# A bidirectional chunked scan: sharing one score product between the two directions

## What is computed

```python
xd = x * dt[..., None]                              # inputs, per head
a_cs = cumsum(dt * a)                               # within a chunk, per head and direction
decay = exp(where(tri, a_cs[:, None] - a_cs[None, :], -inf))
cb = einsum("bclgn,bcsgn->bclsg", cc, bc)           # scores: per group, no direction in them
y_diag = einsum("bclgr,bcsgrp->bclgrp", cb * decay, xd)
states = einsum("bclgn,bclgr,bclgrp->bcgrpn", bc, exp(a_cs[-1] - a_cs), xd)
h = h * exp(a_cs[-1]) + states                      # chunk after chunk, context first
y_off = einsum("bclgn,bcgrpn,bclgr->bclgrp", cc, h_prev, exp(a_cs))
y += y_diag + y_off                                 # both directions are summed
```

## Time and profile before

| | |
|---|---|
| median of 3 runs | 4335.32 us (4332.63 to 4337.5) |
| the profiled execution, its own time | 4333.42 us |
| its span | 4331.6 us |
| mean granted clock of PE over the span | 0.848 |
| busy over the span: PE / DVE / ACT / POOL | 72% / 66% / 26% / 36% |
| the scan stage in the span | from 383.3 us to 560.0 us |
| loads of 1 MB slices within it (L764) | 40 |

### The profile page before, as it was taken

The page is one execution under the profiler, slowest core; times in us unless marked ns, Lnnn a source line. Parts: engine busy times, 40 slices in busy tenths (PEclk is TensorE's granted clock), DMA queues, the critical chain, the costliest instruction groups (busy, mean ns, idle before and its releaser), DMA issues. The chain is left out here.

```text
span 4331.6 us, 38016 instructions
## 1 busy us (share of the span) xinstructions
PE 3116.2 (72%) x12308; PEld 1334.8 (31%) x12308; DVE 2859.9 (66%) x7086; ACT 1130.9 (26%) x2975; POOL 1575.2 (36%) x1383
## 2 busy tenths in 40 slices
PE   8999999866667755555566658999877655555655
PEld 4656554422222211111122113565332211111111
DVE  2524765898888897555555555565888888555554
ACT  1122532333223222111222212563332322111111
POOL 0001413354554454444444441001445455444443
PEclk9999999988878887778778778999888877777677
DMA  4114858999999999999999994105999999999998
GB/s 175 39 39 138 276 187 319 390 420 415 420 420 399 420 421 420 419 421 414 410 419 418 420 417 190 39 1 199 395 420 420 416 421 417 421 421 419 419 421 336
DMA packets 223658, 1471.81 MB, mean 340 GB/s; under 512 B 25436, under 2 KB 29244, under 8 KB 53220
## 3 DMA queue, kind: packets, MB, share of 16 engines
q0 software_dynamic: 184320, 1342.26, 75.0%
q1 hardware_dynamic: 37764, 123.17, 7.9%
q10 hardware_dynamic: 1376, 3.96, 0.2%
HBM read 1467.02 MB, written 2.28 MB: 339 GB/s over the span
## 5 line engine op out<-in xcount | busy, mean ns | idle before, releaser
L1944 PE MATMUL banks<-arena 128*64 128x512 f32 x5120 | 1668.5, 812 | 1159.2 <-ACT arena L2188 1108.6
L1668 POOL DMA_INDIRECT arena<-experts,arena x1280 | 1498.9, 1171 | 2246.5 <-PE banks L1944 1535.3
L2341 DVE CUSTOM_DVE_ANT_0 arena<-arena 128x1024 f32<-128x1024 f32 x1280 | 1537.4, 1223 | 829.5 <-DMA arena<-experts,arena 828.9
L1944 PEld LDWEIGHTS banks<-arena 128*64 128x64 f32 x5120 | 457.5, 185 | 2297.1 <-ACT arena L2188 1295.1
L2182 ACT ACTIVATE arena<-arena 128x4 f32<-128x4 f32 x320 | 66.1, 206 | 2316.9 <-DVE arena L2341 2316.8
L2188 ACT ACTIVATE arena<-arena 128x64 f32<-128x64 f32 x1280 | 340.4, 336 | 37.5 <-DVE arena L2329 0.8
L1759 PE MATMUL banks<-arena 128*128 128x512 f32 (+3 forms) x960 | 289.4, 456 | 6.8 <-DMA arena<-wq 5.7
L442 PE MATMUL banks<-arena 128*128 128x512 f32 (+1 forms) x640 | 208.6, 486 | 0.3 <-PEq L207 0.3
L1759 PEld LDWEIGHTS banks<-arena 128*128 128x128 f32 x960 | 160.8, 191 | 116.3 <-issue 90.8
L879 POOL TENSOR_TENSOR arena<-arena 128x256 f32<-128x256 f32 x48 | 41.1, 856 | 423.5 <-POOLq L633 332.3
L1686 PE MATMUL banks<-arena 128*128 128x512 f32 x416 | 187.9, 600 | 5.9 <-DVE arena L2234 2.1
(11 more groups left out here) (245 smaller groups left out, 2970.5 us busy)
## 6 DMA issues: line engine op xcount, KB each, us to landing
arena<-l_w_ada SPq DMA_DIRECT2D x48, 1024.0 KB, 4.9
arena<-wq SPq DMA_DIRECT2D x54, 512.0 KB, 7.9
arena<-experts,arena POOLq DMA_INDIRECT x1280, 17.3
arena<-l_w_in SPq DMA_DIRECT2D x7, 2048.0 KB, 7.7
arena<-l_w_out SPq DMA_DIRECT2D x4, 1536.0 KB, 8.9
arena<-l_w_o SPq DMA_DIRECT2D x4, 1024.0 KB, 9.2
arena<-keys SPq DMA_DIRECT2D x27, 128.0 KB, 10.4
arena<-gates SPq DMA_DIRECT2D x6, 512.0 KB, 11.9
```

Of the source, the lines that this page charges most:

```text
L1668: pool.indirect_dma_start(slots[n], None, tbl, bass.IndirectOffsetOnAxis(ap=expert[:, ring[c], k:k + 1], axis=0)).then_inc(land[n]["sem"], ...
L1944: mm = pe.matmul(core["ps"][QS * j:QS * j + QS, c, :], diag[:, g % 2, k, :], v[:, D + c * 512:D + (c + 1) * 512], start=(g % (NB * PH) == ...
L2341: dve.tensor_tensor_reduce(u, u, rep[i // PH % 2][:, k % NQ, :], 1.0, 0.0, ALU.mult, ALU.add, dots[:, k:k + 1]).then_inc(dot["sem"], up(dot))
```

## The change

Steps 0 to 23 now do the inner part of both directions: one score product serves two masks, there are two spreads, two decays, two masked copies and two inputs, and the products of the two directions accumulate in PSUM. Steps 24 to 47 keep only the state of the forward direction: L921, L926 and their additions. The cut diff:

```diff
-    E = view(core, RO + 6656, 2, 512)
-    M = view(core, RO + 7680, 2, 512)
-    XD = view(core, RO + 8704, 2, GW)
+    E = view(core, RO + 6656, 4, 512)
+    XD = [view(core, RO + 8704, 2, GW), view(core, C_ONE, 2, GW)]
...
         @block.scalar
+            def decay(n):
+                _r, t, g = steps[n]
+                for j, r in enumerate((1, 0)):
+                    e = E[:, 2 * (n % 2) + j, :]
+                    act.wait_ge(fr["sem"], at(fr, 2 * n + j + 1))
+                    if n >= 2:
+                        act.wait_ge(bk["sem"], at(bk, n - 1))
+                    for h in range(HG):
...
+                    i.then_inc(dd["sem"], up(dd))
+                    act.wait_ge(dd["sem"], at(dd, 2 * n + j + 1))
+                    act.activation(e, e, ACT.Exp, scale=-1.0).then_inc(eo["sem"], up(eo))
+            for n in range(NS):
+                if n < NW:
+                    decay(n)
...
         @block.vector  (mask)
+                dve.wait_ge(fr["sem"], at(fr, 2 * n + 1))
+                for j, r in enumerate((1, 0)):
+                    dve.tensor_tensor(CM[:, 2 * (n % 2) + j, :], core["ps"][:, 2 + n % 2, 0:P], tri[:, r, :],
+                                      ALU.mult).then_inc(cm["sem"], up(cm))
+                for j in range(2):
...
+                    dve.tensor_tensor(e, e, CM[:, b:b + 1, :].to_broadcast([P, HG, P]),
+                                      ALU.mult).then_inc(mo["sem"], up(mo))
...
         @block.vector  (add)
+                state = core["ps"][:, 6 if n < NW else 2 + n % 2, 0:GW]
...
+                if n < NW:
+                    if not opening[n]:
+                        dve.wait_ge(ac["sem"], at(ac, AC[n] + 1))
+                    dve.tensor_tensor(yg, yg, core["ps"][:, 4 + n % 2, 0:GW], ALU.add).then_inc(ac["sem"], up(ac))
...
         @block.gpsimd
+            pool.tensor_tensor(flat(TOE), flat(TOE), flat(DT), ALU.mult).then_inc(xe["sem"], up(xe))
...
+                if n < NW:
+                    for j, a in enumerate((HEADS + c, c)):
+                        pool.tensor_tensor(per(XD[j][:, n % 2, :]), xg, bcast(DT[:, t, a:a + HG], HD),
+                                           ALU.mult).then_inc(xo["sem"], up(xo))
+                if closing[n]:
+                    continue
+                pool.tensor_tensor(per(XE[:, n % 2, :]), xg, bcast(TOE[:, t, a:a + HG], HD),
+                                   ALU.mult).then_inc(xe["sem"], up(xe))
...
         @block.tensor  (front)
                 if n >= 2:
-                    pe.wait_ge(eo["sem"], at(eo, n - 1))
-                    pe.wait_ge(mo["sem"], at(mo, n - 1))
+                    pe.wait_ge(cm["sem"], at(cm, 2 * n - 2))
                 pe.matmul(core["ps"][:, 2 + n % 2, 0:P], bct[:, g, t * P:(t + 1) * P],
                           bct[:, SG + g, t * P:(t + 1) * P], start=True, stop=True)
+                for j, r in enumerate((1, 0)):
+                    e = r * SG + g
+                    if n:
+                        pe.wait_ge(dd["sem"], at(dd, 2 * n - 1 + j))
+                    pe.matmul(core["ps"][:, j, :].rearrange("p (h l) -> p h l", l=P),
...
             front(0)
             for n, (r, t, g) in enumerate(steps):
-                if n + 1 < NS:
+                if n + 1 < NW:
                     front(n + 1)
                 if n == 0:
                     stay_busy(pe, core, 6, 22)
...
+                if n < NW:
+                    pe.wait_ge(mo["sem"], at(mo, 2 * n + 2))
+                    pe.wait_ge(xo["sem"], at(xo, 2 * n + 2))
+                    for h in range(HG):
+                        for j in range(2):
+                            pe.matmul(core["ps"][:, 4 + n % 2, h * HD:(h + 1) * HD],
+                                      E[:, 2 * (n % 2) + j, h * P:(h + 1) * P],
+                                      XD[j][:, n % 2, h * HD:(h + 1) * HD], start=(j == 0), stop=(j == 1))
...
-                    i = pe.matmul(core["ps"][:, 6, 0:GW], br[:, t, g * SN:(g + 1) * SN], XE[:, n % 2, :],
-                                  start=True, stop=True)
+                    i = pe.matmul(core["ps"][:, 6 if n < NW else 2 + n % 2, 0:GW], br[:, t, g * SN:(g + 1) * SN],
+                                  XE[:, n % 2, :], start=True, stop=True)
```

More of the change, by code:

```diff
@@ L727, in ssd_stage @@
     for n in range(NS):
-        AC.append(AC[n] + (2 if opening[n] or closing[n] else 3))
+        AC.append(AC[n] + (1 if opening[n] or closing[n] else 2) + (1 if n < NW else 0))
     gated_at = {n: steps[n][1] for n in range(SG * TT + SG - 1, NS - 1, SG)}
@@ L779, in _ @@
         def _(act):
[L780 to L790, removed]
+            def decay(n):
[6 more added lines that the diff above has]
+                    for h in range(HG):
+                        c = r * HEADS + g * HG + h
+                        i = act.activation(e[:, h * P:(h + 1) * P], core["ps"][:, j, h * P:(h + 1) * P],
+                                           ACT.Relu, bias=KAC[:, t, c:c + 1], scale=-1.0)
+                    i.then_inc(dd["sem"], up(dd))
[4 more added lines that the diff above has]
+                    decay(n)
                 if n - 3 in gated_at:
@@ L840, in add @@
                             out=part(hs, h), in0=part(hs, h), scalar=CD[:, t, c + h:c + h + 1],
-                            in1=part(core["ps"][:, 6, 0:GW], h), op0=ALU.mult, op1=ALU.add)
+                            in1=part(state, h), op0=ALU.mult, op1=ALU.add)
                     i.then_inc(ac["sem"], up(ac))
-                if not opening[n]:
-                    dve.wait_ge(ac["sem"], at(ac, AC[n] + 1))
-                dve.tensor_tensor(yg, yg, core["ps"][:, 4 + n % 2, 0:GW], ALU.add).then_inc(ac["sem"], up(ac))
+                if n < NW:
+                    if not opening[n]:
+                        dve.wait_ge(ac["sem"], at(ac, AC[n] + 1))
+                    dve.tensor_tensor(yg, yg, core["ps"][:, 4 + n % 2, 0:GW], ALU.add).then_inc(ac["sem"], up(ac))
             def gate(u, j):
@@ L889, in front @@
             def front(n):
[L890 removed]
+                _r, t, g = steps[n]
                 if n >= 2:
[L892 to L893 removed]
+                    pe.wait_ge(cm["sem"], at(cm, 2 * n - 2))
                 pe.matmul(core["ps"][:, 2 + n % 2, 0:P], bct[:, g, t * P:(t + 1) * P],
                           bct[:, SG + g, t * P:(t + 1) * P], start=True, stop=True)
[L896 to L900, removed]
+                for j, r in enumerate((1, 0)):
[3 more added lines that the diff above has]
+                    pe.matmul(core["ps"][:, j, :].rearrange("p (h l) -> p h l", l=P),
+                              pick[0:8 * SPLITS, e:e + 1].to_broadcast([8 * SPLITS, P]),
+                              sums[0:8 * SPLITS, :, t * P:(t + 1) * P],
+                              start=True, stop=True).then_inc(fr["sem"], up(fr))
             front(0)
             for n, (r, t, g) in enumerate(steps):
[L904 removed]
+                if n + 1 < NW:
                     front(n + 1)
@@ L912, in _ @@
                     stay_busy(pe, core, 7, 5)
-                pe.wait_ge(mo["sem"], at(mo, n + 1))
-                pe.wait_ge(xo["sem"], at(xo, 2 * n + 2))
                 if n >= 2:
                     pe.wait_ge(ac["sem"], at(ac, AC[n - 1]))
-                for h in range(HG):
-                    i = pe.matmul(core["ps"][:, 4 + n % 2, h * HD:(h + 1) * HD], M[:, n % 2, h * P:(h + 1) * P],
-                                  XD[:, n % 2, h * HD:(h + 1) * HD], start=True, stop=True)
+                if n < NW:
[6 more added lines that the diff above has]
+                                      XD[j][:, n % 2, h * HD:(h + 1) * HD], start=(j == 0), stop=(j == 1))
                 if not opening[n]:
```

42 lines of the change are left out of this document (18 added, 24 removed).

## The result

The median after is 4349.37 us (4347.58 to 4350.81, 7 runs) against 4335.31 us before (4330.48 to 4337.5, 7 runs): a ratio of 1.0029, with a 95% interval of 1.0020 to 1.0039. The change costs 14.06 us; 12.9 had been forecast. By its median it is slower by more than the 0.2% that had been set as the bound; the interval begins at 0.2%. The profiled execution took 4348.66 us, its span is 4346.8 us, and the mean granted clock is 0.847, as before.

A forecast was written before the change was run, and what follows sets the result against it. PE's matmuls were taken to bound the scan steps, with the ring of weight slices late next. The out projection starting 10.2 us later plus clock losses of 1.7 and 1.0 gave +12.9 us, 4348.2 us; range 4333 to 4358.

The forecast's parts named there:

- the likeliest mechanism: Scan stage: PE's matmuls set the backward steps, late weight slices the forward ones; 4348.2 us, chance 0.62.
- Start: Stage start: second spread waits for ACT with 44 busy matmuls queued behind; first products +3.8 us, clock +1.7 us.
- Steps 0 to 23: Backward half: PE sets the step, a full one 4.94 us; 112.6 us from first products to slice 21.
- the ceiling: Steps 0 to 23: an accumulating pair of L918 products costs twice its 0.94 us; the floor was no cost.
- Steps 24 to 47: Forward half: PE's cover is gone, slice loads set 3.02 us a step; slice 39 at 55.45 us after slice 21.
- End: After the last turn: out projection waits for its output weights, L1686 at 570.3 us instead of 560.06, +10.2.
- The turn: Forward half, between groups of slices: row, transpose and columns with handovers take 2.05 us before the next load starts.
- Clock at the opening of the forward half: Idle of 2.5 us ahead of slice 23 lowers the granted clock; +1.0 us, from nothing to 2.4.
- PE is not the bound of the first half: Rival: extra L918 cost little, backward steps fall to the mask's 4.2 us; +0.3 us, 4335.6; chance 0.13.
- The loads are hidden after all: Rival: slices land within two short forward steps, 37.5 us instead of 55.45; -6.1 us, 4329.2; chance 0.06.
- The clock stays down in the forward half: Rival: PE's idle time halves its speed, +1.0 us on some 16 steps, 4364 at most, 4356 likelier; chance 0.13.

The follow-up runs named there:

- the doubled products: Against the kernel after, the backward direction's masked product is made twice in each of the 24 backward steps; 4373.84 us, ratio 1.0088.
- the run of the start: Against the kernel after, the 44 busy matmuls stand ahead of the second step's front instead of behind it; 4347.96 us, ratio 1.0023.
- the kernel with the gates moved: Against the kernel after, DVE's two gate products stand behind the step's row and column work instead of ahead of it; 4354.31 us, ratio 1.0045.
- the third slot: Against the kernel after, a third slot for weight slices from slice 24 on, in the masks' dead buffers; 4346.44 us, ratio 1.0018.
- the four kernels with three slots: Kernel after plus a third slice slot: alone 4346.44 us; with three other edits 4340.16; with slices respread and two other repairs, two forms, 4339.53 and 4336.6.

## Why the prediction was right, step by step

The sum was 12.9 us and 14.06 came; the likeliest mechanism was the one that happened. That the number came so close is in part luck, as the terms show:

- *Start*: 3.8 for ACT and 1.7 for the clock, 5.5 together. The first products came 12.55 us after the first score product instead of 6.46 before (L918 itself starts at 389.80; the 389.69 of the earlier trace rows is its weight load): 6.1. Undoing it gave 5.8. The busy matmuls began 4.1 us later, for ACT, and the fall of the clock was real, 0.57 over 386 to 394: the 44 matmuls took 7.19 us instead of 5.18, 2.0 more.
- *Steps 0 to 23*: 112.6 forecast, 109.4 measured (396.07 to the end of slice 21 at 505.44). A full step is 4.80 instead of 4.94: the pair of products does cost twice the single one (1.84 against 2 x 0.94), as the ceiling had it, while two spreads take 0.53 instead of 0.62. The 14 full steps so give 2.0 of the 3.2 us. The two steps with a turn are 0.45 shorter each than forecast (4.14 and 4.15), and step 0 was given a front that PE had done before it (1.0). Against this the forecast took the front away one step early: `front(23)` is issued in step 22, only step 23 has none, and the two take 8.55 us instead of 7.6. That the step is PE's was shown by the doubled products. The Trainium skill, page "Trainium Kernel Development and Optimization", section Performance Expectations, calls matmul busy time a bad metric for how close a kernel is to roofline, and weight-load busy time a good one. Whether PE sets a step is another question: in the doubled run PE's loads are busy for 34.79 of 50 us, and every added matmul still came out in the time. So the rival that the prediction drew from this rule falls.
- *Steps 24 to 47*: 55.45 forecast from slice 21 to slice 39, 57.7 measured. The 3.02 us a slice were 3.00 in the undisturbed stretch. At slice 31 the forecast still holds within 0.3 us. Then comes the second turn: from the end of slice 31 to that of slice 32 it takes 4.86 us instead of the 3.15 forecast, because DVE wrote its columns late (L158 ends the wait at 539.71). Slice 34, which uses the slot of slice 32, is about as late, PE is idle for 1.98 us ahead of it, and behind that come the low clock, projections of 1.64 and 1.55 us, and slices 4.05 us apart (551.87 to 555.92). So the 2.2 us begin at the turn; that they would not have come without it was not shown. That the ring is the cause of the 3.0 us a slice is shown by leaving 16 loads out. Two slots are the double buffering that the Trainium skill, page "Trainium Kernel Development and Optimization", section Best Practices, advises for overlap of DMA and compute. Here it did not hide a slice whose turn takes 6.05 us behind two steps of 2.06.
- *End*: 8.75 forecast from slice 39 to the out projection, 11.2 measured. **The turn was the term most in error**, here and at the second turn. I took its 2.05 us as the sum of its own operations in the earlier trace rows, with nothing for what DVE has ahead of them in its queue. After, the last turn's row waits behind a gate product on DVE, as its timeline shows, and the turn takes 3.85 us (from the end of slice 39 to 566.97); the second takes 3.79. That is 3.5 us too few in the two. The other 0.6 us of the end come behind the turn: its 20 busy matmuls ran at a low clock, 4.13 us; with the clock at 1.00 (no loads) they took 2.50. And what ends the wait is not what was forecast: the forecast had L1711 released by the DMA of the output weights near 570; it starts at 574.30 and is listed behind the end of the stage (PEq L746), its weight load behind that DMA, up to the same moment (574.27). In the run of the start and in the one without loads, where the 20 matmuls took 2.50 us, the weights do release it, behind 2.24 us of idle time.

```profile
563.82 0.69 DVE L860 TENSOR_TENSOR arena<-arena 128x512 f32<-128x512 f32 x1
564.43 0.68 DVE L876 TENSOR_TENSOR arena<-banks,arena 128x512 f32<-128x512 f32 x1
```

- *Clock at the opening of the forward half*: 1.0 forecast there, none came: 1.00 from 500 to 545 in spite of 2.54 us of idle time ahead of slice 23. This was luck of the run: in the kernel with the gates moved, which does the same up to there, slice 23 took 1.94 us behind 2.40 us of idle time. The loss came later, at 545, 557 and 566, and is counted above.

In sum: 0.6 more at the start, 3.2 less in the backward half, 2.2 more in the forward half, 2.4 more at the end, 1.0 less for the opening: 1.0 more, and 14.1 - 12.9 is 1.2; the rest is rounding and the 0.1 us between the weight load and the product at the start. Errors of both signs nearly cancelled.

The rivals: *PE is not the bound of the first half* falls with the doubled products. *The loads are hidden after all* did not come; its price, 37.5 us from slice 21 to slice 39, was too low as well: with 16 loads left out it is 42.8, since slices 22 and 23 are still loaded there (3.0 of the difference) and the second turn costs 1.7 more. *The clock stays down in the forward half* came in three stretches, not in the whole half.

## What to carry to other kernels

Work that moves from one stage's half to the other leaves behind the transfers that it covered. Before a change evens out the arithmetic, divide the loads over the steps that remain: a step is as long as the longer of its matmuls and its buffer's share of a turn (half of the 6.05 us with two slots). An operation on a wait's path costs its own time and what stands ahead of it in its engine's queue: the turn was 2.05 us by its operations and 3.8 in the queue. And an added wait is to be looked for where the engine's queue behind it is long: here a wait for ACT ahead of 44 filling matmuls cost 6 us at the start of a stage, and moving two lines took 5.8 of them away there.

## What was not expected of the hardware

The granted clock depends on more than the last idle time. In the kernel after it stayed at 1.00 (2.4 GHz) behind 2.54 us of idle time at 510.34; it fell to 0.72 over 545 to 551 behind 1.98 us, and with small matmuls in the waits it still fell at 525 behind 2.29 us. Slice 23 itself (510.34 in the kernel after) was multiplied at half pace with the gates moved and with the third slot, behind 2.40 and 2.69 us. With half of the masked products left out, PE was busy for 91 of 100 us, with short waits between, and 0.91 was granted on the mean, though one profile does not show that the waits are why: the rest of PE's work ran slower, and the time did not move. And the landing of 1 MB is not a constant: its median was 4.9 us in the kernel after (7.6 at most), but 5.0 to 5.9 us in the four kernels with three slots, where more loads can be under way at once.
